# The selection's counts over 640 columns stand in VectorE's order of the scan instead of ScalarE's

## Chip, cores, metric

One core of a Trainium2 chip. The metric is device time in microseconds (us) of one execution of the whole kernel.

## What is computed

One decoder layer for a prompt of 2048 tokens and a group of eight sample tokens. Each layer has a mixer of three parallel head groups, a cross-attention and a gated ConvFFN. Two of the head groups matter here. Group A is sparse attention: an indexer scores every causal key for every query, and each query keeps its 256 best keys:

```
score = einsum('bth,bths->bts', wi * IDX_HEADS ** -0.5, relu(dots))
score = where(visible, score, -inf)
vals, idx = lax.top_k(score, n_sel)
```

Group B is a gated DeltaNet (a recurrence over chunks with a triangular inverse), and group C a Mamba-2 state space scan. B and C do not depend on A.

## The kernel before

The kernel is a chain of stages. `stage_index` writes the scores of the prompt's blocks 2 to 15 (128 queries each, on the 128 partitions) into one tile `sc_score`; block b has 128(b+1) columns, so the first three blocks have 384, 512 and 640. A fifteenth entry holds the sample tokens' scores (8 partitions, 1152 columns as counted).

The threshold of each query, its 256th best score, is found bit by bit: 32 bits, highest first. For each bit, `Selection.propose` sets the bit in a candidate (`sl_cand`) and writes it as a float (`sl_fb`) and as its negative (`sl_nfb`); every block's scores that reach the candidate are counted into `sl_cnt`; `Selection.take` compares the counts with targets and keeps the bit or not (`sl_key`). The 15 entries are in two groups, 0 to 8 and 9 to 14 (`SPLIT`), which go through propose and take apart from each other.

The counting is spread through `stage_scan`, which computes groups B and C in 16 passes, one for each block t of 128 tokens, two bits in each pass. Entries below `HERE` (2 before the change, so 384 and 512 columns) are counted on VectorE by `count_here` (L1801 to L1806): one `tensor_scalar` that compares with `sl_fb`, adds up and writes the comparison to `sn_low`. The others are counted on ScalarE by `count` (L1808 to L1817): a Sign activation with `sl_nfb` as bias, which adds up the signs and writes them to `sn_junk`. The targets of the two kinds differ, and are built from `HERE` on the host.

Within a pass each engine has an order written out by hand (the loops `for t in passes`), and waits on semaphores where an operand comes from another engine:

- ScalarE (L944 to L976) runs the counts of bit 2t, with the scan's small activations between them, then those of bit 2t+1. Between these stand L902 (`sn_B`, a copy that TensorE's L1415 waits for) and L911, L912 (`decays`, which GpSimd's masks L850 `sn_decT` and L846 `sn_dec` wait for). The pass ends with L937 (`sn_ysq`), which waits for VectorE's L1148 `sn_y`.
- VectorE (L1160 to L1255) alternates masks and subtractions of the triangular inverse (L988 `sn_X`, L992 `sn_T`, L996 `sn_TT`, each fed by TensorE and read by it again, in six levels) with the other steps. The places named below are: L1121 `sn_xdt` and behind it L1064 `sn_S` (the DeltaNet state, which waits for TensorE's L1355); and, in the second half of the pass, L1022 `sn_dec` (the clip that ScalarE's L911 waits for), L996, L988, L1138 `sn_H`, L1082 and L1087 (`sn_osb`, the output scaled and gated), L992, and L1037 `sn_attT`, which reads GpSimd's `sn_decT`.
- GpSimd (`block.gpsimd`) does the products with fixed masks and gains, L823 `sn_xd` and L850, L846, L856 among them. SyncE loads the blocks.

```
sel.count(act, 2 * t, HERE, 6)
...
r = PART[g]
...
dve.wait_ge(self.c_act, (NSEL - HERE) * i + r.stop - HERE)
```

The last line is in `take`: VectorE waits there for ScalarE's counts of the group.

Of the kernel before, what the change touches and what calls it, by code (L numbers as in the profile page):

```python
# [143 lines left out]
def bcast(ap, n):  # L144

    return ap.unsqueeze(2).broadcast_to([ap.shape[0], ap.shape[1], n])
# [378 lines left out]
def heads(ap, n):  # L525

    return ap.unsqueeze(1).broadcast_to([ap.shape[0], n, ap.shape[1]])
# [130 lines left out]
def stage_scan(nc, A, gates, masks, sel):  # L658
# [3 lines left out]
    with Scope(nc, "sn") as s:  # L662
# [70 lines left out]
        with nc.Block() as block:  # L733
# [245 lines left out]
            def _(dve):  # L979
# [5 lines left out]
                def masked(t, l):  # L985
                    pl.wait(dve, t, f"x{l}")
                    pl.wait(dve, *((t, f"yt{l - 1}") if l > 1 else (t - 1, "yt6")))
                    vl.done(dve.tensor_tensor(X[:], four(b_a), heads(m(M_LEV + l), 4), ALU.mult), f"X{l}")  # L988
# [5 lines left out]
                def update_TT(t, l):  # L994
                    pl.wait(dve, t, f"yt{l}")
                    vl.done(dve.tensor_tensor(TT[:, t % 2], TT[:, t % 2], four(b_b), ALU.subtract), f"TT{l}")  # L996
# [62 lines left out]
                def state(t):  # L1059
                    pt.wait(dve, t, "s")  # L1060
                    pt.wait(dve, t, "o")
                    ah.wait(dve, t, "er")
                    for a in range(2):
                        ins = dve.scalar_tensor_tensor(S[:, a], S[:, a], er[:, t % 2, a, P - 1:P],  # L1064
                                                       b_m[:, M_S + a * DD:M_S + (a + 1) * DD], ALU.mult, ALU.add)
                    vt.done(ins, "S")

                def raw_out(t):
                    pt.wait(dve, t, "o")
                    pt.wait(dve, t - 1, "flipo")  # L1070
                    for a, bank in enumerate((b_c, b_d)):
                        ins = dve.tensor_scalar(osb[:, a::2], bank[:, 0:2 * DD].rearrange("p (h d) -> p h d", d=DD),
                                                DD ** -0.5, None, ALU.mult)
                    vt.done(ins, "o")
# [32 lines left out]
                def ssd_x(t):  # L1107
                    pq.wait(dve, t, "x")
                    gx.wait(dve, t - 1, "xd")
                    vq.done(dve.tensor_copy(x[:], eight(b_1)), "x")  # L1110
# [7 lines left out]
                def ssd_weigh(t):  # L1118
                    vq.wait(dve, t, "x")
                    pq.wait(dve, t - 1, "y1")  # L1120
                    vq.done(dve.tensor_tensor(xdt[:], x[:], bcast(gcol(t, G_DT, 8), SP), ALU.mult), "xdt")  # L1121
# [13 lines left out]
                def ssd_state(t):  # L1135
                    pq.wait(dve, t, "h")
                    gn.wait(dve, t, "Hd")
                    vq.done(dve.tensor_tensor(H[:], H[:], eight(b_2), ALU.add), "H")  # L1138
# [24 lines left out]
                for t in passes:  # L1163
                    here, nxt, prev = ok(t), ok(t + 1), ok(t - 1)
# [29 lines left out]
                    if here:  # L1194
                        update_TT(t, 2)
                        ssd_x(t)
                        masked(t, 3)
                        ssd_weigh(t)
                    if prev:
                        state(t - 1)  # L1200
                        raw_out(t - 1)
# [19 lines left out]
                        clip(t + 1)  # L1221
                    if here:
                        update_TT(t, 4)
                        masked(t, 5)
                        ssd_state(t)
                    if prev:
# [514 lines left out]
    return score[:, OFF[SEL[n]]:OFF[SEL[n]] + P * (SEL[n] + 1)]  # L1741


HERE, SPLIT = 2, 9
PART = (slice(0, SPLIT), slice(SPLIT, NSEL))


# [1872 lines left out]
```

## Time and profile before

| | |
|---|---|
| device time, median of 3 runs | 4228.36 us (4228.16 to 4229.03) |
| device time of the profiled execution | 4227.98 us |
| its span, first to last instruction | 4225.8 us |
| mean granted TensorE clock | 0.939 |
| busy over the span | TensorE 3811.2, VectorE 2029.6, ScalarE 1677.7, GpSimd 645.8 us |
| the scan with its edges, 990 to 1700 us | 710 us of the span |

PE is TensorE, PEld its weight loads, DVE VectorE, ACT ScalarE, POOL GpSimd, SP SyncE. In the list of waits, the engine and line in front waited for those behind the arrow. In a timeline a number in brackets is the idle time just before an instruction and what ended it; "issue" is time in which the engine waited for nothing that the profile shows. The granted clock is a share of TensorE's full speed: 1.00 is 2.4 GHz, 0.50 is 1.2 GHz.

### The profile page before, as it was taken

How to read it: one execution, taken by the hardware profiler on the slowest of the kernel's cores; microseconds unless marked ns; L12 is line 12 of the kernel's file. 1: busy time of each engine (PE TensorE's matmuls, PEld its weight loads, DVE VectorE, ACT ScalarE, POOL GpSimd, SP SyncE). 2: the span in 40 equal slices, each digit the busy share in tenths (PEclk: the TensorE clock that was granted, in tenths of full speed). 3: DMA queues.
4: the chain of work that ended last, by engine and by line, in shares of the span. 5: the costliest groups of instructions: out<-in, count | busy, mean ns of one | idle time of the engine just before them, and what ended most of it. 6: DMA issues, size and time to landing. Idle time of an engine off the chain costs nothing. (4 is left out here: it accounts for less than half of the span.)

```text
span 4225.8 us, 54267 instructions
## 1 busy us (share of the span) xinstructions
PE 3811.2 (90%) x20428; PEld 3243.9 (77%) x20428; DVE 2029.6 (48%) x3311; ACT 1677.7 (40%) x2904; POOL 645.8 (15%) x395
## 2 busy tenths in 40 slices
PE   8989999686888888599899985799999999799999
PEld 7879999344777777598555553799999999777777
DVE  3245541795999998897377442412112112231111
ACT  5532122685999999265232331211111111131111
POOL 0022211002434443000032000311211211000000
PEclk9999999667999998799999996899999999899999
DMA  3211124501111110510443211111111111242222
GB/s 121 83 59 68 71 102 157 129 6 51 34 42 41 36 47 19 138 43 21 159 125 119 93 36 57 48 42 41 62 41 48 54 41 56 83 155 77 89 78 64
DMA packets 200984, 299.37 MB, mean 71 GB/s; under 512 B 28068, under 2 KB 158940, under 8 KB 188620
## 3 DMA queue, kind: packets, MB, share of 16 engines
q1 hardware_dynamic: 198460, 296.87, 21.5%
q8 instruction: 109, 1.79, 0.2%
q14 instruction: 79, 0.65, 0.0%
q10 hardware_dynamic: 2336, 0.07, 0.0%
HBM read 194.14 MB, written 103.47 MB: 70 GB/s over the span
## 5 line engine op out<-in xcount | busy, mean ns | idle before, releaser
L1816 ACT ACTIVATE sn_junk<-sc_score,sl_nfb 128x640 bf16<-128x640 f32 (+12 forms) x416 | 577.0, 1389 | 0.0
L3228 DVE TENSOR_SCALAR fu_acc<-fu_raw,fu_extra 128x2048 f32<-128x2048 f32 x22 | 28.3, 1286 | 741.5 <-ACT fu_up L3195 741.5
L156 PE MATMUL fu_p_g<-fu_hn_hi,fu_w_hi 128*128 128x412 f32 (+1 forms) x880 | 306.8, 349 | 20.1 <-POOL fu_w_lo L3182 20.1
L156 PE MATMUL fp_p_o<-fp_hn_hi,fp_w_hi 128*128 128x412 f32 (+1 forms) x840 | 294.6, 351 | 18.4 <-POOL fp_w_lo L498 18.4
L156 PE MATMUL fu_p_g<-fu_hn_hi,fu_w_lo 128*128 128x412 f32 (+1 forms) x880 | 309.0, 351 | 0.0
L156 PE MATMUL fu_p_u<-fu_hn_hi,fu_w_lo 128*128 128x412 f32 (+1 forms) x880 | 308.5, 351 | 0.0
L156 PE MATMUL fu_p_g<-all_hn_lo,fu_w_hi 128*128 128x412 f32 (+1 forms) x880 | 307.6, 350 | 0.0
L156 PE MATMUL fu_p_u<-all_hn_lo,fu_w_hi 128*128 128x412 f32 (+1 forms) x880 | 306.8, 349 | 0.0
L156 PE MATMUL fu_p_u<-fu_hn_hi,fu_w_hi 128*128 128x412 f32 (+1 forms) x880 | 306.0, 348 | 0.0
L3330 PE MATMUL fd_p_o<-fd_w_hi,fd_a_hi 128*128 128x512 f32 x680 | 272.2, 400 | 28.6 <-DVE fd_w_lo L3403 28.6
L156 PE MATMUL fp_p_o<-fp_hn_hi,fp_w_lo 128*128 128x412 f32 (+1 forms) x840 | 293.7, 350 | 0.0
L156 PE MATMUL fp_p_o<-h_hn_lo,fp_w_hi 128*128 128x412 f32 (+1 forms) x840 | 292.7, 348 | 0.0
L3331 PE MATMUL fd_p_o<-fd_w_lo,fd_a_hi 128*128 128x512 f32 x680 | 265.4, 390 | 0.0
L3332 PE MATMUL fd_p_o<-fd_w_hi,fd_a_lo 128*128 128x512 f32 x680 | 265.3, 390 | 0.0
L2544 PE MATMUL mc_p_mix<-wt_w_out,mc_mix 128*128 128x512 f32 x512 | 240.3, 610 | 20.2 <-DMA wt_w_out<-in_w_out 11.1
L3180 POOL TENSOR_TENSOR fu_w_hi<-fu_w,fu_one 128x2048 fp32r<-128x2048 f32 x22 | 84.0, 3817 | 751.2 <-DMA fu_w<-in_w_gu 751.2
L3195 ACT ACTIVATE fu_up<-fu_p_u 128x412 f32<-128x412 f32 (+1 forms) x110 | 56.5, 514 | 353.5 <-PE fu_p_u L156 353.5
L418 ACT ACTIVATE fp_raw<-fp_p_o 128x412 f32<-128x412 f32 (+1 forms) x105 | 53.8, 512 | 359.6 <-PE fp_p_o L156 294.5
L3195 ACT ACTIVATE fu_raw<-fu_p_g 128x412 f32<-128x412 f32 (+1 forms) x110 | 56.7, 516 | 342.6 <-PE fu_p_g L156 290.2
L2544 PEld LDWEIGHTS mc_p_mix<-wt_w_out,mc_mix 128*128 128x128 f32 x512 | 93.6, 194 | 124.4 <-issue 120.7
L156 PEld LDWEIGHTS fu_p_g<-fu_hn_hi,fu_w_hi 128*128 128x128 f32 x880 | 165.7, 188 | 20.8 <-POOL fu_w_lo L3182 20.5
L3330 PEld LDWEIGHTS fd_p_o<-fd_w_hi,fd_a_hi 128*128 128x128 f32 x680 | 128.2, 189 | 59.2 <-issue 32.9
(508 smaller groups left out, 8785.0 us busy)
## 6 DMA issues: line engine op xcount, KB each, us to landing
scratch_act<-fu_acc SPq DMA_DIRECT2D x22, 1088.0 KB, 4.9
fu_w<-in_w_gu SPq DMA_DIRECT2D x22, 1024.0 KB
fd_a<-scratch_act SPq DMA_DIRECT2D x34, 640.0 KB, 4.6
scratch_conv<-fp_acc SPq DMA_DIRECT2D x14, 1028.0 KB, 3.9
scratch_halves<-fp_acc_lo SPq DMA_DIRECT2D x14, 1024.0 KB, 7.6
fp_w<-in_w_fm SPq DMA_DIRECT2D x21, 512.0 KB
scratch_tm<-np_out SPq DMA_DIRECT2D x17, 524.0 KB, 2.7
np_x<-in_x SPq DMA_DIRECT2D x17, 512.0 KB, 4.0
```

The costliest lines, as they stand in the source:

```text
L156: last = pe.matmul(out, a, b, start=k == 0, stop=k == n - 1)
L418: act.activation(raw[:, i.u, 3 + at:3 + at + n], ps[:, c, 0:n], ACT.Copy).then_inc(c_raw, 1)
L1816: act.activation(self.junk[0:p, j % 2, 0:w], src, ACT.Sign, bias=self.nfb[0:p, n:n + 1].bitcast(F32), accum_out=self.cnt[0:p, n:n + 1]).th ...
L2544: last = pe.matmul(p_mix[:, c], mix[:, t % 2, k], wo[:, k, bass.ts(c, CHUNK)], start=k == 0, stop=k == KT - 1)
L3180: pool.tensor_tensor(hi, a, one[:].broadcast_to([P, 2 * G]), ALU.mult).then_inc(c_split, 1)
L3195: act.activation(dst, bank[:, 0:n], ACT.Copy).then_inc(c_cp, 1)
L3228: dve.tensor_scalar(a, raw[:, 2:2 + SEQ], taps(i.t, 2), None, ALU.mult)
L3330: pe.matmul(ps[:, t % 2, c], a_hi[:, j % RING, i], w_hi[u][:, i, n], start=f == 0, stop=False)
L3331: pe.matmul(ps[:, t % 2, c], a_hi[:, j % RING, i], w_lo[u][:, i, n], start=False, stop=False)
L3332: last = pe.matmul(ps[:, t % 2, c], a_lo[:, j % RING, i], w_hi[u][:, i, n], start=False, stop=False)
```

## The change

`HERE` becomes 3. So entry 2, with 640 columns, leaves ScalarE's counts (their loops and the waits of `take` follow from `HERE`) and is counted by `count_here` at two new places of VectorE's order: for bit 2t behind `ssd_weigh` (L1121), ahead of the state (L1064); for bit 2t+1 behind the fourth level's `update_TT` (L996), ahead of the fifth level's mask (L988). The tile `sn_low` grows from 512 to 640 columns, and `sl_fb` is written for three entries instead of two. Nothing else changes.

```diff
@@ VectorE's order of stage_scan
                         ssd_x(t)
                         masked(t, 3)
                         ssd_weigh(t)
+                    if here:
+                        sel.count_here(dve, 2)
                     if prev:
                         state(t - 1)
                         raw_out(t - 1)
@@
                     if here:
                         update_TT(t, 4)
+                        sel.count_here(dve, 2)
                         masked(t, 5)
                         ssd_state(t)
@@
-HERE, SPLIT = 2, 9
+HERE, SPLIT = 3, 9
```

What VectorE has in a row ahead of the state's update, one of the passes, before (all names are tiles; `sn_p_m` and its like are PSUM banks of the scan):

```order
L988 TENSOR_TENSOR sn_X<-sn_p_la,all_masks 128x512
L1121 TENSOR_TENSOR sn_xdt<-sn_x,mx_gates 128x512
L1064 SCALAR_TENSOR_TENSOR sn_S<-sn_S,sn_er,sn_p_m 128x64 x2
L1072 TENSOR_SCALAR sn_osb<-sn_p_c 128x2x64
L1072 TENSOR_SCALAR sn_osb<-sn_p_d 128x2x64
```

and now:

```order
L988 TENSOR_TENSOR sn_X<-sn_p_la,all_masks 128x512
L1121 TENSOR_TENSOR sn_xdt<-sn_x,mx_gates 128x512
L1808 TENSOR_SCALAR sn_low,sl_cnt<-sc_score,sl_fb 128x640
L1064 SCALAR_TENSOR_TENSOR sn_S<-sn_S,sn_er,sn_p_m 128x64 x2
L1072 TENSOR_SCALAR sn_osb<-sn_p_c 128x2x64
L1072 TENSOR_SCALAR sn_osb<-sn_p_d 128x2x64
```

The count of bit 2t (L1808 is the L1805 of before, three lines further down) stands between the product and the state. In the second half of the pass VectorE has now:

```order
L1022 TENSOR_SCALAR sn_dec<-sn_dec 128x512
L996 TENSOR_TENSOR sn_TT<-sn_TT,sn_p_lb 128x512
L1808 TENSOR_SCALAR sn_low,sl_cnt<-sc_score,sl_fb 128x640
L988 TENSOR_TENSOR sn_X<-sn_p_la,all_masks 128x512
L1138 TENSOR_TENSOR sn_H<-sn_H,sn_p_s 128x512
L1082 TENSOR_TENSOR sn_osb<-sn_osb,sn_st 128x256
L1087 TENSOR_TENSOR sn_osb<-sn_osb,sn_gate 128x256
L992 TENSOR_TENSOR sn_T<-sn_T,sn_p_la 128x512
L1037 TENSOR_TENSOR sn_attT<-sn_p_c,sn_decT 128x2x128
```

Before, the same rows stand there without the count. On ScalarE, where the counts of bit 2t+1 begin, before:

```order
L907 ACTIVATE sn_osq<-sn_osb 128x256
L897 ACTIVATE sn_df<-sn_df 128x1024
L1816 ACTIVATE sn_junk,sl_cnt<-sc_score,sl_nfb 128x640
L1816 ACTIVATE sn_junk,sl_cnt<-sc_score,sl_nfb 128x768
L1816 ACTIVATE sn_junk,sl_cnt<-sc_score,sl_nfb 128x896
```

and now:

```order
L1819 ACTIVATE sn_junk,sl_cnt<-sc_score,sl_nfb 8x1152
L907 ACTIVATE sn_osq<-sn_osb 128x256
L897 ACTIVATE sn_df<-sn_df 128x1024
L1819 ACTIVATE sn_junk,sl_cnt<-sc_score,sl_nfb 128x768
L1819 ACTIVATE sn_junk,sl_cnt<-sc_score,sl_nfb 128x896
```

The count over 640 columns is gone from the head of the bit's counts, as from that of bit 2t in each pass; whatever ScalarE runs behind it in the pass stands one or two counts nearer to its start.

## Rows read from the trace of the kernel before

**Rows 1.** Busy time by engine: stretch, length, then PE, PEld, DVE, ACT, POOL (us), clock, DMA.
```profile
990.00:1700.00 710.00, 595.37 (x4430) 530.24 (x4430) 627.93 (x1446) 666.91 (x1070) 279.71 (x270) 0.94 0.12 36
```

**Rows 2.** The list of waits, 990 to 1690 us: total us, times, longest us.
```profile
ACT sn_ysq L937 <- DVE sn_y L1148: 19.0, 11, 3.7
...
DVE sn_S L1064 <- PE sn_p_d L1355: 15.2, 15, 1.0
...
DVE sn_attT L1037 <- issue: 4.4, 5, 0.9
```

**Rows 3.** ScalarE: its group of the 640 columns, then two starts of L937 (timeline).
```profile
L1816 ACT ACTIVATE sn_junk<-sc_score,sl_nfb 128x640 bf16<-128x640 f32 x32 | 26.0, 813 | 0.0
...
1342.53 0.63 ACT L937 ACTIVATE sn_ysq<-sn_y 128x512 f32<-128x512 f32 x1
...
1386.51 0.63 ACT L937 ACTIVATE sn_ysq<-sn_y 128x512 f32<-128x512 f32 x1 [2.14 <-DVE sn_y L1148]
```

**Rows 4.** VectorE: the counts' two groups, then one count and its follower (timeline).
```profile
L1805 DVE TENSOR_SCALAR_CACHE_REDUCE sn_low<-sc_score,sl_fb 128x512 bf16<-128x512 f32 x32 | 23.7, 739 | 0.0
...
L1805 DVE TENSOR_SCALAR_CACHE_REDUCE sn_low<-sc_score,sl_fb 128x384 bf16<-128x384 f32 x32 | 19.4, 605 | 0.0
...
1309.75 0.74 DVE L1805 TENSOR_SCALAR_CACHE_REDUCE sn_low<-sc_score,sl_fb 128x512 bf16<-128x512 f32 x1
...
1310.41 0.69 DVE L1158 COPY sn_yT<-sn_p_s 128x512 f32<-128x512 f32 x1
```

**Rows 5.** Timeline before the state's update, VectorE and GpSimd (start us, duration us).
```profile
1355.45 1.17 DVE L1121 TENSOR_TENSOR sn_xdt<-sn_x,mx_gates 128x512 f32<-128x512 f32 x1
1357.65 0.47 DVE L1064 SCALAR_TENSOR_TENSOR sn_S<-sn_S,sn_er,sn_p_m 128x64 f32<-128x64 f32 x2 [1.03 <-PE sn_p_d L1355]
...
1356.03 1.49 POOL L823 TENSOR_TENSOR sn_xd<-sn_x,sn_skip 128x512 f32<-128x512 f32 x1
```

**Rows 6.** Timeline of a pass where ScalarE is late: VectorE, ScalarE, GpSimd.
```profile
1328.98 0.42 DVE L1022 TENSOR_SCALAR sn_dec<-sn_dec 128x512 f32<-128x512 f32 x1
...
1331.11 0.42 DVE L1082 TENSOR_TENSOR sn_osb<-sn_osb,sn_st 128x256 f32<-128x256 f32 x1
...
1333.45 0.42 DVE L1037 TENSOR_TENSOR sn_attT<-sn_p_c,sn_decT 128x256 f32<-128x256 f32 x1 [0.86 <-issue]
...
1330.88 0.61 ACT L911 ACTIVATE sn_dec<-sn_dec 128x512 f32<-128x512 f32 x1
...
1332.09 1.27 POOL L850 TENSOR_TENSOR sn_decT<-sn_decT,all_masks 128x512 f32<-128x512 f32 x1 [5.49 <-ACT sn_decT L912]
```

**Rows 7.** The same place in a pass where ScalarE is early; first a group.
```profile
L1082 DVE TENSOR_TENSOR sn_osb<-sn_osb,sn_st 128x256 f32<-128x256 f32 x15 | 10.4, 696 | 0.0
...
1372.28 0.42 DVE L1022 TENSOR_SCALAR sn_dec<-sn_dec 128x512 f32<-128x512 f32 x1
...
1374.40 1.11 DVE L1082 TENSOR_TENSOR sn_osb<-sn_osb,sn_st 128x256 f32<-128x256 f32 x1
1375.55 1.38 DVE L1087 TENSOR_TENSOR sn_osb<-sn_osb,sn_gate 128x256 f32<-128x256 f32 x1
...
1377.44 0.41 DVE L1037 TENSOR_TENSOR sn_attT<-sn_p_c,sn_decT 128x256 f32<-128x256 f32 x1
...
1373.96 1.27 POOL L850 TENSOR_TENSOR sn_decT<-sn_decT,all_masks 128x512 f32<-128x512 f32 x1 [4.05 <-ACT sn_decT L912]
1375.19 1.45 POOL L846 TENSOR_TENSOR sn_dec<-sn_dec,all_masks 128x512 f32<-128x512 f32 x1
```

**Rows 8.** TensorE's timeline in the last pass.
```profile
1673.17 2.05 PE L1415 MATMUL sn_p_s<-sn_xw,sn_B 128*128 128x256 f32 x4 [3.63 <-ACT sn_B L902]
```

**Rows 9.** VectorE behind TensorE at the lower clock (timeline), and the busy times there.
```profile
1359.19 0.69 DVE L992 TENSOR_TENSOR sn_T<-sn_T,sn_p_la 128x512 f32<-128x512 f32 x1 [0.66 <-PE sn_p_la L1321]
...
1360.89 0.69 DVE L996 TENSOR_TENSOR sn_TT<-sn_TT,sn_p_lb 128x512 f32<-128x512 f32 x1 [1.02 <-PE sn_p_lb L1327]
...
1357.70:1361.10 3.40, 3.40 (x18) 3.31 (x17) 1.72 (x6) 3.40 (x5) 0.54 (x1) 0.50 0.00 0
```

## The prediction

> **What bounds the kernel now.** The change lies in one stage, so I read the busy times of the stretch from 990 to 1700 us first. VectorE is busy for 627.93 of its 710 us, ScalarE for 666.91, TensorE for 595.37 [rows 1]. By shares alone ScalarE looks like the bound, and 32 counts taken from it like a gain. The list of waits says otherwise: ScalarE waits 19.0 us in 11 of 16 passes, at the end of the pass, for VectorE's `sn_y` [rows 2]; it is VectorE that arrives last there. VectorE's own waits are put down to TensorE (15.2 us for the state, about 1.0 in each of 15 passes), and five of them, of 0.9 each at most, to "issue" at `sn_attT` [rows 2]. Those five are ScalarE's only hold that I find on the way to the end. In the pass of rows 6 ScalarE is late: it begins L911 at 1330.88, though VectorE's clip was done at 1328.98 + 0.42 = 1329.40; GpSimd's mask therefore begins at 1332.09 and ends at 1333.36, and `sn_attT` begins at 1333.45 after 0.86 us of idleness [rows 6]. So the path of a pass is VectorE and TensorE by turns, with a detour over ScalarE and GpSimd in five passes.
>
> In six other passes ScalarE had caught up. There GpSimd's masks begin early and meet VectorE: L1082, 0.42 us where GpSimd is idle [rows 6], takes 1.11 beside L850, and L1087 1.38 beside L846 [rows 7]. Six of 1.11 and nine of 0.42 make the group's 10.4 us [rows 7], which gives the six. From the end of the clip to the start of `sn_attT` it is 1333.45 - 1329.40 = 4.05 us with ScalarE late, and 1377.44 - 1372.70 = 4.74 with it early [rows 6, 7]: an early ScalarE costs VectorE 0.69 us.
>
> **Off ScalarE.** 32 activations of 813 ns go, 26.0 us in all or 1.63 in each pass [rows 3]; their accumulator reads lie under the next activation. Worth in itself: nothing where ScalarE then waits longer for `sn_y`. In the five late passes it removes the 0.86 of idleness and puts the meeting with GpSimd in its place. In the last pass TensorE waits 3.63 us for ScalarE's `sn_B` [rows 8]; both counts stand ahead of it, so up to 1.63 come back there, part of it eaten by the second count.
>
> **On VectorE, one count.** 512 columns take 739 ns, 384 take 605 [rows 4], so 640 should take 739 + 134 = 873 ns. The instruction behind a count starts 0.08 before the count's end (1309.75 + 0.74 against 1310.41) [rows 4]; a count thus occupies 0.79 us, 25.3 us for 32. The Trainium skill (page "VectorE: DVE Perf Modes", section "The perf-mode tier table (the rule you actually need)") lets a `tensor_scalar` on fp32 in SBUF run at two elements a cycle. L1022, 512 columns in 0.42 us [rows 6], agrees with that, and the count's 739 ns for as many columns does not; by the rule a count would occupy an estimated 0.41, and the sum below would come out at its lower end. I go by the count's own rows.
>
> **The first count** stands behind L1121, which ends at 1355.45 + 1.17 = 1356.62, and ahead of the state, which starts at 1357.65 because TensorE's products are done only then [rows 5]. 1356.62 + 0.79 = 1357.41 is before that. TensorE is not waiting for VectorE at this place, so the idle 1.03 us take the count and the price is nothing, in 15 passes. The cover is thin (0.24 us). In the first pass there is no state to wait for: between 0 and 0.8, I take 0.4.
>
> **The second count** delays L988, L1138, and with them L1082 and L1087, by 0.79. ScalarE is now early in every pass, so each looks like rows 7 with a count in it: GpSimd's L850 runs from 1.26 after the clip's end (1373.96), L846 from 2.49 (1375.19) [rows 7]. L1082 came at 1374.40 and lost its time waiting for L850; with the count it comes at 1374.40 + 0.79 = 1375.19, the very moment at which L846 starts. This is the open place of the sum.
> - If VectorE gets in first, L1082 no longer waits, L1087 waits for L846 as before, and `sn_attT` starts about 4.8 us after the clip: the count was hidden in the waiting.
> - If GpSimd gets in first, both wait for one GpSimd operation more. I price that at one more meeting, 1.11 - 0.42 = 0.69: `sn_attT` starts at about 5.5.
>
> Nothing tells the two orders apart, so I take the middle, 5.15. Against 4.74 that is +0.41 in each of the six early passes (2.5), against 4.05 it is +1.10 in each of the five late ones (5.5), and for three further passes, in which neither shows, the mean of both (3 x 0.75 = 2.3). With +0.4 for the first pass and -0.8 for the last (the middle of 0 and -1.6) the sum is 2.5 + 5.5 + 2.3 + 0.4 - 0.8 = **+9.9 us**. Its ends: 6 x 0.06 + 5 x 0.75 + 3 x 0.4 - 1.6 = +3.7, and 6 x 0.75 + 5 x 1.44 + 3 x 1.1 + 0.8 = +15.8.
>
> What else moves: the waits of `take` for ScalarE's counts get shorter; no DMA is added or moved; `sl_fb` with three columns for two changes no row that I can price.
>
> The profiled execution took 4227.98 us (span 4225.8, 2.2 outside it), 0.4 less than the median of 4228.36. With the sum it makes 4237.9, and on the scale of the median **4238.3**; ends 4232 and 4244.
>
> **Rivals.**
> 1. *ScalarE was the bound after all, and the kernel gets faster.* For it: 666.91 of 710 busy, and five passes in which ScalarE waits for nothing. Then these five shrink by 1.63 each and the last pass by 1.6: 4228.4 - 8.2 - 1.6 = 4218.6. It decides if VectorE in such a pass has 1.63 us to give beside the two counts, that is if its waits for TensorE give way when TensorE gets `sn_B` sooner. Against it: the only hold found is the 0.86 at `sn_attT`, and as soon as that goes, GpSimd's masks meet L1082. Chance 0.09.
> 2. *The first count is not hidden.* L823 on GpSimd runs from 1356.03 to 1357.52 [rows 5], over the whole place of the count. If the count must let it finish, as L1082 must, it ends at 1357.52 + 0.79 = 1358.31, and the state starts 0.66 late in 15 passes: +9.9 on top, 4248.2. The Trainium skill (page "SBUF — State Buffer", section "SBUF: two separate sides") says that a VectorE operation in a two-port mode, or with two SBUF inputs, and a GpSimd operation shut each other out for a whole instruction; L1082 with its two inputs agrees [rows 7]. Against it: the counts of before, many of them beside GpSimd's work, average 739 ns for 512 columns and 605 for 384 [rows 4], and a single meeting of the kind of L1082 would add 0.69. Chance 0.10.
> 3. *TensorE's clock.* At 1357.70 to 1361.10 the granted clock is 0.50 (1.2 GHz), and VectorE waits 0.66 at `sn_T` and 1.02 at `sn_TT` [rows 9]. Six passes have this second wait; TensorE went through the small products of L1355 without a gap before it fell. The clock's falls do not stand still when the pass gets longer. If all six passes were spared, 6 x 1.68 = 10.1 would come back: 4228, no change. If four more were hit, 4245. For it: pass lengths change by 0.4 to 1.1 us. Against: they change little, and nothing in the change aims at the products. Chance of a time within 8 us of before by this way: 0.16.
>
> **How the numbers follow.** The forecast has 0.65, the rivals 0.09, 0.10 and 0.16. About 0.2%, 8.5 us, is what a measurement of this kernel can tell from no change; slower by more is above 4236.8. Of the forecast's stretch from 4232.1 to 4244.2 some 0.6 lies above that: 0.65 x 0.6 = 0.39, with rival 2 0.49. Faster is rival 1, 0.09; the rest, 0.26 + 0.16 = 0.42, is no change. The range, 4228 to 4247, holds the forecast with its ends and the upper half of rival 3, and leaves out rival 1 and most of rival 2.
>
> **What would show it.** Right: ScalarE's group of 640 columns gone and its wait for `sn_y` grown in every pass to several us; the count of 640 near 873 ns; the wait at `sn_S` down from 1.03 to about 0.2 and `sn_S` still at the same distance from `sn_y`; no "issue" wait at `sn_attT`; L1082 or L1087 long in every pass, with `sn_attT` 4.8 to 5.5 us behind the clip. The order at GpSimd's switch shows in L1082: near 0.5 us if VectorE got in, above 1.2 if not. Wrong: passes that shrink by over 1 us, an `sn_S` that starts late behind a long count, or a different number of passes with the 1.02 at `sn_TT`.

## The result and the profile after

The change takes **4268.12 us** (median of 4 runs, 4261.35 to 4272.31) where the kernel before took 4228.26 beside it: a ratio of 1.0094, interval 1.0082 to 1.0106, or 40 us more. The forecast was 4238.3, its range ended at 4247. The profiled execution took 4264.44 with a span of 4262.7; the mean granted clock fell from 0.939 to 0.929.

The busy times of the scan after (990 to 1740 us; it ends some 34 us later than before), to be read against [rows 1]:

```profile
990.00:1740.00 750.00, 632.33 (x4436) 567.50 (x4435) 661.60 (x1512) 642.02 (x1006) 280.31 (x270) 0.89 0.12 35
```

VectorE has 33.7 us more work, 25.3 of which the forecast had counted; ScalarE has 24.9 less. TensorE executes the same products, and is busy for 37 us more at a clock of 0.89 where it was 0.94. That is the first sign that much of the time is not VectorE's. VectorE's groups of the counts and of L1082 say that the two operations themselves are as forecast [rows 4, 7]:

```profile
L1808 DVE TENSOR_SCALAR_CACHE_REDUCE sn_low<-sc_score,sl_fb 128x640 bf16<-128x640 f32 x32 | 27.8, 869 | 0.0
...
L1082 DVE TENSOR_TENSOR sn_osb<-sn_osb,sn_st 128x256 f32<-128x256 f32 x16 | 21.3, 1328 | 0.6 <-ACT sn_st L932 0.6
```

The list of waits of after, 990 to 1690 us:

```profile
ACT sn_ysq L937 <- DVE sn_y L1148: 67.9, 14, 5.4
...
DVE sn_X L988 <- PE sn_p_lb L1330: 30.0, 13, 2.9
...
PE sn_p_c L1292 <- DVE sn_kv L1009: 22.0, 15, 1.8
...
DVE sn_TT L996 <- PE sn_p_lb L1330: 8.0, 15, 1.0
...
PE sn_p_s L1418 <- ACT sn_B L902: 5.9, 9, 2.0
...
DVE sn_S L1064 <- PE sn_p_d L1358: 3.0, 13, 0.2
```

and three rows of the same list of the kernel before, which did not stand ahead of the prediction:

```profile
PE sn_p_s L1415 <- ACT sn_B L902: 25.9, 16, 3.6
...
PE sn_p_c L1289 <- DVE sn_kv L1009: 8.2, 7, 1.3
...
DVE sn_X L988 <- PE sn_p_lb L1327: 5.7, 3, 2.4
```

ScalarE waits for `sn_y` in 14 passes, and `sn_S` waits 0.2 us where it waited 1.0: both as forecast. Not forecast are the three rows in the middle. TensorE's wait for `sn_B` is down from 25.9 to 5.9 us; in its place it waits 22.0 us for `sn_kv` instead of 8.2; and VectorE waits 30.0 us, up to 2.9 in a pass, at `sn_X` behind TensorE's L1330, where it waited 5.7 behind the same product (L1327 there). One pass shows how they hang together, first TensorE's timeline, then VectorE's:

```profile
1298.18 1.05 PE L1310 MATMUL sn_p_la<-sn_T,sn_AT 128*128 128x128 f32 x8
...
1303.70 1.77 PE L1324 MATMUL sn_p_la<-sn_X,sn_TT 128*128 128x128 f32 x8 [1.40 <-DVE sn_X L988]
1305.27 3.52 PE L1426 MATMUL sn_p_s<-sn_xdt,sn_df 128*128 128x64 f32 x16
1308.57 2.02 PE L1310 MATMUL sn_p_la<-sn_T,sn_AT 128*128 128x128 f32 x8
1310.39 1.30 PE L1330 MATMUL sn_p_lb<-sn_TT,sn_X 128*128 128x128 f32 x8
```

```profile
1301.23 0.42 DVE L1022 TENSOR_SCALAR sn_dec<-sn_dec 128x512 f32<-128x512 f32 x1
...
1304.16 1.53 DVE L1082 TENSOR_TENSOR sn_osb<-sn_osb,sn_st 128x256 f32<-128x256 f32 x1
...
1307.08 0.41 DVE L1037 TENSOR_TENSOR sn_attT<-sn_p_c,sn_decT 128x256 f32<-128x256 f32 x1
...
1311.80 0.69 DVE L988 TENSOR_TENSOR sn_X<-sn_p_la,all_masks 128x512 f32<-128x512 f32 x1 [1.81 <-PE sn_p_lb L1330]
```

and the busy times around it (PE is the second number, the clock the third from the end):

```profile
1299.30:1303.90 4.60, 1.46 (x17) 1.27 (x18) 4.55 (x12) 3.08 (x6) 0.99 (x1) 1.00 0.02 4
1303.90:1310.70 6.80, 6.80 (x34) 6.80 (x34) 6.05 (x13) 6.80 (x10) 2.38 (x3) 0.51 0.07 19
```

Eight products of L1310 take 1.05 us at 1298.18 and 2.02 at 1308.57. In between TensorE was busy for 1.46 of 4.60 us, and from 1303.90 its granted clock is at the lower of its two levels (0.51 over 6.80 us; 0.50 is 1.2 GHz). L1426 takes 3.52 us; in the kernel before it is L1423 and takes 1.90 (below). By the time that L1330 is done, VectorE has waited 1.81 us. The same place in a pass of the kernel before, 28.5 to 33.1 us behind that pass's `sn_y` as here:

```profile
1328.50:1333.10 4.60, 4.22 (x44) 3.91 (x42) 4.06 (x9) 4.60 (x8) 1.01 (x1) 1.00 0.02 3
```

There TensorE is busy for 4.22 of 4.60 us, and keeps its clock. Its idle time lies a little earlier, in front of the step that waits for ScalarE:

```profile
1327.09 1.10 PE L1415 MATMUL sn_p_s<-sn_xw,sn_B 128*128 128x256 f32 x4 [2.07 <-ACT sn_B L902]
1328.03 1.05 PE L1307 MATMUL sn_p_la<-sn_T,sn_AT 128*128 128x128 f32 x8
1329.01 0.37 PE L1289 MATMUL sn_p_c<-sn_qk 64*128 64x128 f32 x1
...
1331.65 1.90 PE L1423 MATMUL sn_p_s<-sn_xdt,sn_df 128*128 128x64 f32 x16
```

With ScalarE late, TensorE waits 2.07 us for `sn_B`, runs L1415 and L1307 behind it, and finds `sn_kv` ready. With ScalarE early it runs them at once and then waits for `sn_kv`, and behind those short products for `sn_X`, which the second count delays. The pass shown has a lower clock earlier too, at the place of [rows 9]; in the passes of the change without that, TensorE waits 0.45 for `sn_B` and 1.3 for `sn_kv`, and the clock falls all the same in all but one.

Below, **place P** is the one of [rows 9] (a lower clock that begins 15 to 17 us behind `sn_y`, behind the small products of the outputs) and **place Q** this one (it begins 30 to 35 us behind `sn_y`). A stretch at the lower clock is called a fall. A pass is the time between two starts of L1148, the first 14 passes of the scan are compared, and falls are counted from the granted clock of each trace:

| kernel | pass without a fall | mean of 14 | falls at P, Q | last pass |
|---|---|---|---|---|
| before | 41.83 | 43.08 | 6, 2 | 40.90 |
| the change | 43.19 | 45.83 | 6, 13 | 36.19 |

Five passes of the kernel before have no fall at all (three have one 27 to 28 us into the pass, and take 0.1 to 0.8 more), and of the change only one. Here are the starts of such a pass and of the next, first before, then in the change (41.83 and 43.19 us):

```profile
1299.98 0.69 DVE L1148 TENSOR_TENSOR sn_y<-sn_y,sn_z 128x512 f32<-128x512 f32 x1
...
1341.81 0.69 DVE L1148 TENSOR_TENSOR sn_y<-sn_y,sn_z 128x512 f32<-128x512 f32 x1
```

```profile
1181.80 0.69 DVE L1148 TENSOR_TENSOR sn_y<-sn_y,sn_z 128x512 f32<-128x512 f32 x1
...
1224.99 0.69 DVE L1148 TENSOR_TENSOR sn_y<-sn_y,sn_z 128x512 f32<-128x512 f32 x1
```

So 14 x 2.75 = 38.5 us more, 4.7 less in the last pass, and 2.9 more behind the last `sn_y`: 36.7 of the span's 36.9 (these are the two profiled executions; the medians differ by 40). The stretch behind the last `sn_y`, which no edit in this document touches, takes 2534.6 to 2548.2 us in the traces of all its kernels, so the 2.9 say nothing about the change, and kernels whose totals differ by a few us are better told apart by their passes. The 38.5 are two terms: the pass itself is longer by 1.36 (19.0 in 14), and the falls cost 14 x 2.64 = 37.0 instead of 14 x 1.25 = 17.5, that is 19.5 more.

### The profile page after: what moved, and what is told of

The parts are those of the page before. It is cut to its first block and busy times, and to the rows that moved or that the text cites. A ratio compares the mean times of both kernels' runs of the same rounds, so it can differ in the third digit from the quotient of the medians.

```text
span 4262.7 us, 54267 instructions
## 1 busy us (share of the span) xinstructions
PE 3851.3 (90%) x20428; PEld 3283.0 (77%) x20428; DVE 2062.1 (48%) x3375; ACT 1653.5 (39%) x2840; POOL 647.0 (15%) x395
## 5 line engine op out<-in xcount | busy, mean ns | idle before, releaser
L1819 ACT ACTIVATE sn_junk<-sc_score,sl_nfb 128x768 bf16<-128x768 f32 (+11 forms) x384 | 551.0, 1437 | 0.2 <-DVE sl_nfb L1801 0.2
```

The source lines that it names most:

```text
L1819: act.activation(self.junk[0:p, j % 2, 0:w], src, ACT.Sign, bias=self.nfb[0:p, n:n + 1].bitcast(F32), accum_out=self.cnt[0:p, n:n + 1]).th ...
```

## First round: which half of the move costs

Three theories stood at first. T: the second count on VectorE makes TensorE's waits longer, and the clock falls behind them. E: an early ScalarE costs by itself. W: it is VectorE's added work as such.

**No count of 640 columns at all.** ScalarE is as early as in the change, VectorE has nothing added.

```diff
                         ssd_weigh(t)
-                    if here:
-                        sel.count_here(dve, 2)
...
                         update_TT(t, 4)
-                        sel.count_here(dve, 2)
```

`take` waits for two counts of VectorE instead of three, and the key of the block with 640 columns is preset; both are left out above.

> This kernel leaves out the 32 counts over 640 columns on both engines, so the selection of the block with 640 columns is not found. Theory T: the second count lengthens the stretch in which TensorE waits for VectorE, TensorE's clock falls behind it in 14 passes, and sn_X waits 1.8 to 2.9 us there. Without the counts the falls go and only the early ScalarE is left, which meets GpSimd's masks in every pass: 4228 to 4237, long waits of sn_X for sn_p_lb in 2 to 4 passes. Rival E: the early ScalarE alone (sn_B and the decays sooner) makes the falls: 4258 to 4272. Rival W: VectorE's 25 us of added work simply add up: 4228 or less.

Measured: 4234.15 us, ratio 1.0014 (1.0004 to 1.0024), as T had it. Early ScalarE alone costs little, but not nothing: 4 of 14 passes have a fall at Q, and a pass without a fall takes 42.52, 0.69 more than before, which is what the prediction read for an early ScalarE.

**Both engines count.** ScalarE keeps its two counts, VectorE makes them too, into a spare column.

```diff
-HERE, SPLIT = 3, 9
+HERE, SPLIT = 2, 9
...
-                          accum_out=self.cnt[:, n:n + 1]).then_inc(self.c_here, 1)
+                          accum_out=self.cnt[:, n:n + 1] if n < HERE else self.spare[:]).then_inc(self.c_here, 1)
```

> ScalarE keeps its 32 counts over 640 columns, and VectorE makes both of them as well (into a spare column that nobody reads). Theory T: what VectorE has to do sets the pass, ScalarE's work of 41.7 us a pass fits under the longer pass, so it comes out like the changed kernel, 4255 to 4272, with sn_X waiting for sn_p_lb in most passes. Rival E: with ScalarE's load unchanged it does not run ahead, so few falls: 4230 to 4245. Rival W: 4253, half a per cent, without falls.

Measured: 4222.45, ratio 0.9993 (0.998 to 1.0005). T and W missed by over 30 us, and E's range by 8. In total the same 32 counts at the same places cost nothing that can be measured as long as ScalarE has its own work: the pass without a fall is longer by 0.79, one count's time, and the falls at P and Q that the kernel before has are gone. Two rows of its list of waits show what is different:

```profile
PE sn_p_s L1418 <- ACT sn_B L902: 35.8, 16, 3.6
...
DVE sn_X L988 <- PE sn_p_lb L1330: 2.7, 1, 2.7
```

The wait for `sn_B` is there, and no pass has a fall at P or Q; all 14 take 42.1 to 42.8 us (six have a fall 27 to 28 us into the pass, which costs at most 0.1).

**The second count one step later**, behind the fifth level's mask.

```diff
-                        sel.count_here(dve, 2)
                         masked(t, 5)
+                        sel.count_here(dve, 2)
```

> The second count stands one step later, behind the fifth level's mask (sn_X) that TensorE waits for, instead of ahead of it; all else as in the change. Theory T: TensorE no longer waits 0.8 longer, the falls become few, the meeting with GpSimd's masks stays: 4236 to 4246, sn_X waiting for sn_p_lb in at most 5 passes. Rivals E and W: nothing changes, 4258 to 4272.

Measured: 4241.65, ratio 1.0036 (1.0021 to 1.005). The time is as T expected; the trace is not, with waits of 0.7 to 1.1 at `sn_X` in 12 passes and a fall in each of these, seven at Q and five just behind it (35.2 to 35.6 us).

**Dummy products at Q.** Nine products of 128 columns that nobody reads, five behind L1310 and four behind the products of `sn_kv`.

```diff
                         level_x(t, 5)
+                        fill(t, 5)
...
                     if here:
+                        fill(t, 4)
                         level_y(t, 5)
```

> The change, with nine extra products of two masks on TensorE in each pass, five ahead of the pair products of the next block and four ahead of the fifth level's second product, into a bank that is free there; VectorE, ScalarE and GpSimd are as in the change. Theory T: TensorE is busy where it waited, the clock does not fall, sn_X does not wait: 4234 to 4246, granted clock of the scan up from 0.89. Rivals E and W: time as the change's, 4258 to 4275.

Measured: 4239.28, ratio 1.0027 (1.0015 to 1.0038). Work added to TensorE makes the kernel 29 us faster than the change. No fall at Q is left, but 10 at P.

## Second round: one count, and ScalarE's order

My theory was then that both an early ScalarE and the second count are needed, and that GpSimd's masks, which come early with ScalarE's `decays`, carry part of it.

**The second count alone moved**, the first left to ScalarE.

```diff
                         ssd_weigh(t)
-                    if here:
-                        sel.count_here(dve, 2)
...
-                        sel.count(act, 2 * t, HERE, 6)
+                        sel.count(act, 2 * t, sel.lo(2 * t), 6)
```

`sel.lo` gives `HERE - 1` for bit 2t and `HERE` for bit 2t+1. The targets and `take`'s waits follow from that.

> Only the count of bit 2t+1 stands in VectorE's order; that of bit 2t stays in ScalarE's, so ScalarE is early by half as much. Theory C (an early ScalarE and the second count together gather TensorE's waits into one stretch, behind which its granted clock falls): about half of the change's loss or more, 4242 to 4262, with waits of sn_X for L1330 in 4 to 14 passes and L1082 at 1.1 us or more in most. Rival S (the second count alone, whatever ScalarE does): 4258 to 4270. Rival D (both counts are needed, the first one counts too): under 4238.

Measured: 4268.68, ratio 1.0086 (1.0073 to 1.0099): all of the loss, as rival S had it and above what theory C allowed, with 13 falls at Q.

**ScalarE's order, three kernels:** `decays` one count further back, `sn_B` one count further back, and both.

```diff
+                    if here:
+                        sel.count(act, 2 * t + 1, SPLIT, 10)
                     if nxt:
                         decays(t + 1)
                         state_rows(t + 1)
                     if here:
-                        sel.count(act, 2 * t + 1, SPLIT, 13)
+                        sel.count(act, 2 * t + 1, 10, 13)
```

```diff
-                        ssd_B(t)
                         sel.count(act, 2 * t + 1, 6, 7)
+                        ssd_B(t)
```

> The change, with ScalarE's decays and state rows one count (of the second group) further back, sn_B where it is. Theory C in the form that GpSimd's masks are what an early ScalarE costs: L1082 back at 0.42, sn_attT under 5 us behind the clip, time 4235 to 4250. Rival B (it is sn_B being early that moves TensorE's products and its waits): L1082 0.42 too, but sn_X still waits 1.8 us or more for L1330 in 10 passes or more, time over 4255. If ScalarE's exponentials now come too late, sn_attT has an issue wait of up to 1 us a pass and the time is 4240 to 4255 by that way.

> The change, with ScalarE's copy of sn_B one count (768+128 columns) further back, decays where they are. Rival B: sn_X's waits for L1330 fall to under 1 us, L1082 stays at 1.53, time 4235 to 4250. Theory C in the form of the masks: waits at sn_X nearly as in the change, 4258 to 4272.

> The change, with both sn_B and the decays one count further back, which is about where an unchanged ScalarE has them. Theory C: as the kernel with both counts on VectorE and on ScalarE, 4218 to 4232, L1082 0.42 in nearly all passes and no falls that cost. Rival S (it is the second count on VectorE): over 4250. If only one of the two matters, this is within 6 us of the better of the two kernels that move one.

Measured: 4272.77 (ratio 1.01, 1.0085 to 1.0114), 4259.15 (1.0069, 1.0045 to 1.0094) and 4262.38 (1.0077, 1.0064 to 1.009). Theory C in the form of the masks fell: late `decays` bring nothing (L1082 is back at 0.42 in only 4 of 14 passes, and these take 45.8 us, as in the change), and in the first kernel rival B's time and waits held, with 12 waits of 1.8 us or more at `sn_X` and 14 falls at Q. But rival B's time for the second kernel missed as well (4259.15 for 4235 to 4250; waits at `sn_X` in 5 passes), and the third agreed with rival S alone, which the kernel with counts on both engines had refuted. The trace of the second one was the most telling: eight of its 14 passes take 43.2 us, TensorE waits 1.67 for `sn_B` in these and they have no fall; five take 46.3 to 47.5, and those have a fall at P *and* one at Q. In these TensorE waits 0.05 at most for `sn_B` and 1.5 to 1.8 for `sn_kv`: a fall at P makes TensorE late, `sn_B` is then there before it, and the idle time gathers at Q again. To see Q by itself, P had to go.

## Third round: TensorE kept busier at both places

For P, the eight products of level 3 are put between the halves of the outputs' small products, and VectorE's `update_T(t, 3)` ahead of the state to match. For Q, the nine dummy products stay.

```diff
                     if prev:
-                        outputs(t - 1)
+                        outputs(t - 1, 0)
                     if here:
                         level_y(t, 3)
+                    if prev:
+                        outputs(t - 1, 1)
+                    if here:
                         level_yt(t, 3)
...
+                    if here:
+                        update_T(t, 3)
                     if prev:
                         state(t - 1)
                         raw_out(t - 1)
                     if here:
-                        update_T(t, 3)
                         update_TT(t, 3)
```

**The change with both edits.**

> The change, with the same two edits on TensorE. Theory F: passes near 43.2 throughout, 14 x 2.64 = 37 us come back of the change's time, 4224 to 4236, so that the change is still 14 to 22 slower than the kernel before with the same edits. L1082 stays at 1.1 or more. Rival (the order of the work itself costs the loss): 4250 or more. If the interleaving lengthens a pass by itself: both kernels by the same amount.

Measured: **4228.46**, ratio 1.0001 (0.9992 to 1.0011). No fall at either place; the passes take 43.25. The 40 us of the change are back, though ScalarE is as early as it was and VectorE still makes both counts. The half of the sentence on the kernel before with these edits did not come true (below).

**The same with `sn_B` and `decays` late.**

> The change with sn_B and the decays one count further back on ScalarE, and with the same two edits on TensorE. Theory F: passes near 42.6 (the second count's 0.79 and no meeting with GpSimd's masks), 4217 to 4229, between the kernel before and the change with these edits. Rival (the masks' meeting costs nothing once the clock holds): within 4 us of the change with these edits.

Measured: 4227.87, ratio 0.9998 (0.9989 to 1.0007). The passes take 42.67, 0.58 less than in the kernel above (one has a fall, at 35.9 us, and takes 44.82); the last pass takes 38.17 instead of 36.27. Both forecasts have the total in their range, within 4 us of the kernel above as the rival said, but the rival's reason, that the masks' meeting costs nothing, fails on the passes. The two traces say that the scan from the first `sn_y` to the last is 3.0 us shorter, which the totals do not resolve. They also hold the two orders between which the prediction could not choose. VectorE in this kernel (`sn_B` and `decays` late):

```profile
1291.97 0.42 DVE L1024 TENSOR_SCALAR sn_dec<-sn_dec 128x512 f32<-128x512 f32 x1
...
1292.90 0.87 DVE L1822 TENSOR_SCALAR_CACHE_REDUCE sn_low<-sc_score,sl_fb 128x640 bf16<-128x640 f32 x1
...
1294.90 0.42 DVE L1084 TENSOR_TENSOR sn_osb<-sn_osb,sn_st 128x256 f32<-128x256 f32 x1
...
1295.35 1.38 DVE L1089 TENSOR_TENSOR sn_osb<-sn_osb,sn_gate 128x256 f32<-128x256 f32 x1
...
1297.26 0.41 DVE L1039 TENSOR_TENSOR sn_attT<-sn_p_c,sn_decT 128x256 f32<-128x256 f32 x1
```

and in the one above:

```profile
1290.42 0.42 DVE L1022 TENSOR_SCALAR sn_dec<-sn_dec 128x512 f32<-128x512 f32 x1
...
1291.35 0.87 DVE L1820 TENSOR_SCALAR_CACHE_REDUCE sn_low<-sc_score,sl_fb 128x640 bf16<-128x640 f32 x1
...
1293.35 1.54 DVE L1082 TENSOR_TENSOR sn_osb<-sn_osb,sn_st 128x256 f32<-128x256 f32 x1
...
1294.93 0.83 DVE L1087 TENSOR_TENSOR sn_osb<-sn_osb,sn_gate 128x256 f32<-128x256 f32 x1
...
1296.28 0.41 DVE L1037 TENSOR_TENSOR sn_attT<-sn_p_c,sn_decT 128x256 f32<-128x256 f32 x1
```

From the end of the clip to `sn_attT` it is 4.87 us with VectorE first (the scaled output in 0.42) and 5.44 with GpSimd first (1.54); forecast were 4.8 and 5.5.

**The kernel before with both edits.**

> The kernel before, without the change, but with TensorE kept busier at the two places where its clock falls: the eight products of level 3 stand between the first and the second half of the output's small products (VectorE's update of T goes ahead of the state to match), and nine dummy products stand around the products of sn_kv. Theory F: nearly no falls that cost, passes near 41.8, no wait of 1.02 at sn_TT; 14 passes x 1.25 = 17.5 us come back, 4206 to 4218. Rival (the falls are a result of VectorE's waits and not their cause, so that filling TensorE's time gives nothing): 4225 to 4240.

Measured: 4240.08, ratio 1.003 (1.002 to 1.004): a miss, and in the wrong direction. The rival's time is met at its edge, but not its reason: P and Q have no falls, and it is a third place, 27 to 29 us into the pass, that has 12 (the kernel before has 3 there, in passes that take 0.1 to 0.8 more); and a pass without one takes 42.4, so the dummy products alone cost some 0.6 where TensorE has no idle time for them.

**The first count alone moved.**

```diff
                         update_TT(t, 4)
-                        sel.count_here(dve, 2)
...
-                        sel.count(act, 2 * t + 1, HERE, 6)
+                        sel.count(act, 2 * t + 1, sel.lo(2 * t + 1), 6)
```

Here `sel.lo` gives `HERE - 1` for bit 2t+1 and `HERE` for bit 2t.

> Only the count of bit 2t stands in VectorE's order; that of bit 2t+1 stays in ScalarE's. Theory F (the loss is two terms: the second count with GpSimd's masks makes a pass without a fall of TensorE's clock longer, 41.83 to 43.19, and the falls make up the rest): the first count lies in the state's wait, passes without a fall stay at 41.8 to 42.5, the wait at sn_S is 0.23, time 4222 to 4240. Rival (an early ScalarE alone brings the loss): over 4245.

Measured: 4230.55, ratio 1.0006 (0.9996 to 1.0015). Passes without a fall take 41.83 as before: the first count is free.

## Fourth round: one edit at a time

**The change with the interleaving at P alone** (the diff of the third round, without the dummy products; so too in the next two).

> The change with the interleaving at level 3 alone (no dummy products). If the falls at the second place follow from those at the first: passes near 43.2, 4224 to 4236. If they are independent: no wait of 1.02 at sn_TT any more, but sn_X still waits 1.8 to 2.9 for L1330 in several passes, and the time is 4240 to 4262.

Measured: 4246.33, ratio 1.0047 (1.0034 to 1.006). No fall at P, 7 at Q: Q's falls do not need those at P, as the second forecast had it, but there were 13 with them. The 6 that are gone are as many as the passes of the change that had a fall at both places.

**The kernel before with the interleaving at P alone.**

> The kernel before with the interleaving at level 3 alone. If its falls at the first place cost it what its trace shows: passes of 41.8 to 42, 4208 to 4220. If removing falls at one place brings them up at a third (as with both edits, 27 to 29 us into the pass): 4225 to 4240.

Measured: 4214.51, ratio 0.9972 (0.9961 to 0.9983). The falls of the kernel before at P cost what its trace showed; its mean pass is 42.01. A pass without a fall takes 41.85, so the interleaving costs nothing by itself.

**The first count moved, with the interleaving at P.**

> Only the first count moved, with the interleaving at level 3. The count fills the state's wait; ScalarE is early by 0.8 us a pass. If the fall at the first place goes and none comes in its place: 4206 to 4220, faster than both kernels. If falls come up elsewhere: 4222 to 4240.

Measured: **4212.2**, ratio 0.9961 (0.9948 to 0.9975), faster than the kernel before and than the change, though not by a margin that tells it from the interleaving alone (0.9972, 0.9961 to 0.9983). All passes but the first and the last take 41.9, and of the first 14 none has a fall:

```profile
990.00:1690.00 700.00, 576.03 (x4436) 507.64 (x4436) 642.23 (x1491) 654.79 (x1039) 281.94 (x270) 0.97 0.13 38
```

TensorE is busy for 576 us in this stretch, which holds the whole scan, with the work that took it 595 before and 632 in the change.

**The change, with one more small operation on VectorE at the end of each pass.**

```diff
                         update_TT(t, 6)
+                        sel.pad(dve, 1)
```

> The change with one more operation on VectorE at the end of each pass (0.42 us, some 0.34 occupied), which nobody waits for and which computes nothing that is used. If the falls come from the order of the work alone: 15 x 0.34 = 5 us more than the change, 4270 to 4278. If the length of the pass decides which passes are hit: another number of passes with falls, and a time more than 8 us away from that, most likely below (a pass of the change without a fall would make 43.2 + 0.34).

Measured: 4275.13, ratio 1.0115 (1.0099 to 1.013). That is what the order of the work alone gives. The falls lie in other passes (8 at P, 11 at Q), but the sum is moved by no more than the added work. So I cannot say which passes are hit, only at which places.

## Fifth round: the time of `sn_B` alone

Over all kernels up to here, 8 of 109 passes in which TensorE waited more than 1 us for `sn_B` had a fall at Q, and 78 of the 143 others. Six of the eight are passes of the kernel with the second count alone, which wait 1.27 us for `sn_B`. A count is no experiment, so two kernels move this one copy, with P mended in both.

**The change with the interleaving, and `sn_B` one count later** (the second ScalarE edit above).

> The change with the interleaving at level 3, and ScalarE's copy of sn_B one count further back; no dummy products. If it is the missing wait for sn_B that gathers TensorE's idle time at the second place: TensorE waits 1.6 us for sn_B in each pass, no or few falls there, passes near 43.2, 4222 to 4234. If the second count alone makes them: falls in about 7 of 14 passes as without the late sn_B, 4240 to 4252.

Measured: 4232.21, ratio 1.0012 (1.0002 to 1.0021), 14 us less than with `sn_B` early, without a dummy product. Three rows of its list of waits:

```profile
PE sn_p_s L1420 <- ACT sn_B L902: 29.8, 16, 3.5
...
DVE sn_X L988 <- PE sn_p_lb L1331: 1.2, 1, 1.2
...
PE sn_p_c L1293 <- DVE sn_kv L1009: 1.1, 2, 0.8
```

TensorE waits for `sn_B` in every pass, no longer for `sn_kv`, and Q has no fall in 14 passes, each of 43.2 after the first.

**The kernel before with the interleaving, and `sn_B` two counts earlier** (and ahead of the two small activations of `norm_out`). VectorE has no added count here.

```diff
-                        sel.count(act, 2 * t + 1, HERE, 6)
+                        sel.count(act, 2 * t + 1, HERE, 4)
+                        ssd_B(t)
+                        sel.count(act, 2 * t + 1, 4, 6)
```

> The kernel before (both counts on ScalarE) with the interleaving at level 3, and ScalarE's copy of sn_B two counts nearer to the start, so that TensorE waits for it by 2 us less. If the missing wait is enough by itself: falls at the second place in several passes, waits of sn_X for L1327's successor, 4222 to 4245. If it takes the second count on VectorE too: none, 4207 to 4222, as with sn_B in its place.

Measured: 4233.17, ratio 1.0017 (1.0008 to 1.0026), 19 us more than with `sn_B` in its place, for an operand that is ready sooner:

```profile
PE sn_p_c L1291 <- DVE sn_kv L1010: 30.2, 16, 2.4
...
DVE sn_X L989 <- PE sn_p_lb L1329: 22.2, 9, 2.9
```

and in one pass the busy times at the place:

```profile
1289.00:1292.70 3.70, 1.50 (x17) 1.31 (x18) 3.67 (x10) 3.70 (x7) 0.00 (x0) 0.97 0.00 0
...
1295.50:1302.00 6.50, 6.50 (x31) 6.50 (x32) 3.31 (x10) 6.50 (x9) 3.65 (x4) 0.50 0.01 2
```

8 of 14 passes have a fall at Q, and the picture of the change is there without the change: TensorE busy for 1.50 of 3.70 us, then the lower clock, then 2.9 us of waiting at `sn_X`. The missing wait is enough by itself for falls at Q in these 8.

It is not the whole of the change's 13, as the traces of the rounds above show. The table has six of the kernels without the interleaving, and only their passes without a fall at P, so that Q stands by itself (the wait is that of most passes):

| kernel | second count on VectorE | wait for `sn_B`, us | passes with a fall at Q |
|---|---|---|---|
| no count of 640 columns at all | no | 0.45 | 4 of 10 |
| first count alone moved | no | 1.25 | 0 of 7 |
| the change | yes | 0.45 | 7 of 8 |
| second count alone moved | yes | 1.27 | 6 of 7 |
| the change, `sn_B` late | yes | 1.67 | 0 of 9 |
| the change, `sn_B` and `decays` late | yes | 1.70 | 2 of 8 |

At much the same wait, 1.25 and 1.27, the second count decides: it delays the `sn_X` that TensorE waits for next. So the falls at Q come from the two together, an early `sn_B` and the second count.

## Why the prediction was wrong

**The step that failed is "Off ScalarE", with rival 3.** The prediction put the freed ScalarE time at nothing except in the last pass, and rival 3 priced TensorE's clock at P alone (1.68 a pass, "if four more were hit, 4245"), because "nothing in the change aims at the products". The change does aim at them: an earlier `sn_B` takes away TensorE's wait of about 2 us in front of L1415, the same idle time then lies at Q, right ahead of the wait for `sn_X` that the second count makes longer (1.80 and 1.40 us around one group of short products in the pass shown), and behind these the clock falls in 13 of 14 passes. The prediction followed the second count's delay of L988 to VectorE's next steps, and not to TensorE, which waits for L988. The last kernels show that the time of `sn_B` turns Q's falls on (0 to 8) and off (7 to 0). The size at P was short as well: the pass of [rows 7, 9], with a fall at P alone, takes 43.98 us, 2.15 more than one without, where the prediction added two waits to 1.68. P kept its six falls; the sign that I named for the clock, another number of passes with 1.02 at `sn_TT`, would not have shown any of it.

**The first count** is free, as forecast: `sn_S` waits 0.2, and the kernel with that count alone keeps passes of 41.83. Rival 2 fell:

```profile
1331.51 1.49 POOL L823 TENSOR_TENSOR sn_xd<-sn_x,sn_skip 128x512 f32<-128x512 f32 x1
1332.02 0.87 DVE L1808 TENSOR_SCALAR_CACHE_REDUCE sn_low<-sc_score,sl_fb 128x640 bf16<-128x640 f32 x1
```

The count takes its 0.87 us in the midst of GpSimd's L823. The Trainium skill (page "SBUF — State Buffer", section "SBUF: two separate sides") names two-port modes and operations with two SBUF inputs as those that are shut out; the count has one SBUF tensor, shows no fast mode (869 ns) and is not held; L1082 has two and takes 1.53 beside GpSimd's mask, so trace and page agree.

**The count's length** was right: 873 forecast, 869 measured. The Trainium skill (page "VectorE: DVE Perf Modes", section "The perf-mode tier table (the rule you actually need)") would have let it occupy an estimated 0.41 us; the rows decide against it for a `tensor_scalar` that also accumulates.

**The second count with GpSimd** went to the upper of the two forecast orders, 5.44 us from clip to `sn_attT` in nearly all passes against 4.06 in a late pass before: 1.38 where 1.44 was the upper price and the middle was taken. Both parts of it can be seen by themselves: the count without the masks' meeting makes the pass 0.79 longer (both engines count, 42.62), the meeting without the count 0.69 (no count at all, 42.52), and the two together 1.36. But the prediction charged the six "early" passes of before a smaller step, from 4.74. These passes were the ones with a fall at P (43.98 us in [rows 7, 9]): ScalarE was early there because a slower TensorE had held VectorE back. Against a pass without a fall, each of the 14 pays 1.36, 19.0 in all instead of the forecast's 10.3 before the last pass. This is the second error, and it alone would have stayed inside the range, since the **last pass** gave 4.7 instead of 0.8. That was luck, for the prediction had at most 1.6 there, and with its 0.8 the sum would lie at the range's end: TensorE's wait for `sn_B` shrank from 3.63 to 2.28 us, and the lower clock lasted 3.4 us instead of 13.7. Why it ended sooner was not tried.

**Rival 1** fell: ScalarE's wait for `sn_y` grew to 67.9 us.

The sum as it came out: +19.0 for the second count and the masks, +19.5 for the falls, -4.7 in the last pass, +2.9 behind it, of which the last is inside the spread of that stretch.

## What to carry to other kernels

Before an operand is made earlier for an engine that waits for it, look at what that engine does next: if its next wait is for another engine, the idle time does not go, it gathers. On TensorE that cost the clock here: waits of 2.07 and 0.38 us, with the products of L1415, L1307 and the short ones between them, left it at 1.00; waits of 1.80 and 1.40 around one group of short products did not. When passes of one loop differ in length, find the undisturbed passes first and price a change against those; a state seen only in disturbed passes is a result of the disturbance and no base. And where a step is relieved, follow every operand that it issues, not only the one on the path of today.

## What the runs showed that I had not expected

- Work that computes nothing made the kernel faster: nine dummy products took the change from 4268 to 4239, and the kernel in which ScalarE counted too, so that VectorE's 32 counts were superfluous, took 4222.
- A fall outlasts the gap ahead of it: TensorE was busy for 1.46 of 4.60 us from 1299.3 to 1303.9, ran at half its clock until 1310.7 though it was busy without a gap in between, and VectorE paid at `sn_X`, 8 us behind the gap.
- Edits against falls are not additive. Dummy products and interleaving together gave the change 40 us, and made the kernel before 13 slower, which the interleaving alone made 11 faster: TensorE there had no idle time for the dummies, and falls at a third place grew from 3 to 12. Why they came up there was not tried.
- What stays open is which passes are hit. In the change two pass lengths alternate (45.8 with a fall at Q alone, 46.3 with one at each place); with one more small operation on VectorE the pattern is another, at the same sum but for the added work.
